# Fifteen more turns by block transposes and DRAM trips in a two-block transformer kernel, and the last down slots by token tile

## What is computed

```python
q, k, v, f_logit = split(h @ w_in)                     # fox_mixer: 16 heads of 128
cum = cumsum(log_sigmoid(f_logit + b_f))
s = (rms_norm(q) @ rms_norm(k).T) * scale + (cum_q - cum_k)
h = h + causal_softmax(s) @ v @ w_out
up = conv3(rms_norm(h) @ w_up); gate, val = split(up)
h = h + (silu(gate) * val) @ w_down                    # width 5632

z = rms_norm(h) @ w_in_2                               # second block
o = hgrn2_scan(silu(hq) * dk**-0.5, 1 - g, hi, log(g)) # 8 heads of 128, g = lb + (1 - lb) * sigmoid(hf)
y_a = rms_norm(o) * silu(hg)
y_b = chunk_band_attention(aq, ak, av, rel_bias)       # 16 heads of 64
merged = gate_a * (y_a @ w_branch_a) + gate_b * (y_b @ w_branch_b)
h = h + merged @ w_out_2
h = h + square(relu(rms_norm(h) @ w_up_2)) @ w_down_2
return rms_norm(h)
```

## Time and profile before

| | us |
|---|---|
| median of 3 runs (lowest, highest) | 2573.26 (2572.63, 2573.35) |
| profiled execution | 2572.82 |
| its span, first to last instruction | 2570.6 |
| PE busy | 2545.2 (99%) |
| DVE busy | 1628.3 (63%) |
| ACT busy | 1274.0 (50%) |
| mean granted TensorE clock | 0.998 of full speed |
| DMA | 530.04 MB, 206 GB/s |

### The profile page before, as it was taken

The page is one execution under the profiler, slowest core; times in us unless marked ns, Lnnn a source line. Parts: engine busy times, 40 slices in busy tenths (PEclk is TensorE's granted clock), DMA queues, the critical chain, the costliest instruction groups (busy, mean ns, idle before and its releaser), DMA issues.

```text
span 2570.6 us, 32628 instructions
## 1 busy us (share of the span) xinstructions
PE 2545.2 (99%) x11604; PEld 2114.7 (82%) x11604; DVE 1628.3 (63%) x1812; ACT 1274.0 (50%) x1609; POOL 173.9 (7%) x289
## 2 busy tenths in 40 slices
PE   8999999999999999999999999999999999999998
PEld 7888888888888888878888888888888888888886
DVE  5666655766666666666677555455565666666665
ACT  5555554655555555554343645454444444444444
POOL 0111100100000000000001000000010000000000
PEclk9999999999999999999999999999999999999999
DMA  7877756877777777755556666665677777777775
GB/s 227 257 204 220 204 170 203 241 225 225 226 223 227 223 223 228 207 170 174 157 151 188 209 194 184 181 191 185 187 238 212 222 211 221 213 219 217 215 219 156
DMA packets 264773, 530.04 MB, mean 206 GB/s; under 512 B 20747, under 2 KB 22131, under 8 KB 264563
## 3 DMA queue, kind: packets, MB, share of 16 engines
q1 hardware_dynamic: 243488, 469.82, 60.7%
q0 software_dynamic: 17152, 54.54, 7.7%
q10 hardware_dynamic: 4051, 4.59, 0.5%
HBM read 501.07 MB, written 27.81 MB: 206 GB/s over the span
## 4 chain that ended last, share of the span: by engine, by line
PE 97%; DVE 1%; DMA 1%; ACT 1%; issue 0%; POOL 0%; ACTq 0%; POOLq 0%; SPq 0%
PE acc L449 31%; PE acc L451 31%; PE acc L450 31%; PE acc L704 1%; PE acc L462 1%; PE acc L557 1%; PE acc L564 0%; DMA scratch<-qk_rows 0%; DVE w_lo L1323 0%; PE acc L579 0%; DVE scratch L1533 0%; DMA raw<-in_w 0%; ACT w_hi L855 0%; PE acc L580 0%; PE acc L741 0%
## 5 line engine op out<-in xcount | busy, mean ns | idle before, releaser
L1323 DVE TENSOR_TENSOR w_lo<-raw,w_hi 128x1024 fp32r<-128x1024 f32 x887 | 1080.4, 1222 | 813.8 <-ACT w_hi L855 811.1
L855 ACT ACTIVATE w_hi<-raw 128x1024 fp32r<-128x1024 f32 x887 | 938.6, 1060 | 1060.3 <-PE acc L451 1001.0
L449 PE MATMUL acc<-w_hi,A_hi 128*128 128x512 f32 x1948 | 769.1, 395 | 0.8 <-issue 0.8
L451 PE MATMUL acc<-w_hi,A_lo 128*128 128x512 f32 x1948 | 758.7, 389 | 0.0
L450 PE MATMUL acc<-w_lo,A_hi 128*128 128x512 f32 x1948 | 758.7, 389 | 0.0
L451 PEld LDWEIGHTS acc<-w_hi,A_lo 128*128 128x128 f32 x1948 | 365.7, 188 | 76.9
L449 PEld LDWEIGHTS acc<-w_hi,A_hi 128*128 128x128 f32 x1948 | 365.9, 188 | 75.8 <-issue 1.4
L450 PEld LDWEIGHTS acc<-w_lo,A_hi 128*128 128x128 f32 x1948 | 365.9, 188 | 73.8
L449 PE MATMUL acc<-w_hi,B_hi 128*128 128x512 f32 x800 | 313.9, 392 | 3.1 <-issue 3.1
L451 PE MATMUL acc<-w_hi,B_lo 128*128 128x512 f32 x800 | 312.1, 390 | 0.0
L450 PE MATMUL acc<-w_lo,B_hi 128*128 128x512 f32 x800 | 311.8, 390 | 0.0
(11 more groups left out here) (184 smaller groups left out, 1240.2 us busy)
## 6 DMA issues: line engine op xcount, KB each, us to landing
raw<-in_up SPq DMA_DIRECT2D x304, 512.0 KB, 4.2
raw<-in_w SPq DMA_DIRECT2D x271, 512.0 KB, 4.1
raw<-in_down SPq DMA_DIRECT2D x216, 512.0 KB, 4.6
raw<-in_wo SPq DMA_DIRECT2D x64, 512.0 KB, 3.9
up_rows<-scratch POOLq DMA_DIRECT2D x21, 512.0 KB, 5.1
scratch<-up_rows POOLq DMA_DIRECT2D x84, 128.0 KB, 5.1
raw<-in_wa SPq DMA_DIRECT2D x16, 512.0 KB, 4.9
raw<-in_wb SPq DMA_DIRECT2D x16, 512.0 KB, 4.7
```

The costliest lines, as they stand in the source:

```text
L449: pe.matmul(o, hi[:, kt, ts], wh, start=first and kk == 0, stop=False)
L451: m = pe.matmul(o, lo[:, kt, ts], wh, start=False, stop=last and kk == SLOT_K - 1)
L855: act.activation(w_hi[:, q % RING, :], raw[:, q % RING, :], ACT.Copy).then_inc(w_hi_ready, 1)
L1323: dve.tensor_tensor(w_lo[:, q % RING, :], raw[:, q % RING, :], f32(w_hi[:, q % RING, :]), ALU.subtract).then_inc(w_lo_ready, 1)
```

## The change

1. Fifteen turns leave PE and go by trips through `turn_rows`: three of the new residual in wo1, the six of the decayed attention, three merged chunks and three of the second residual (`BY_BLOCK`). The sources are ordinary tiles, so DVE cuts the blocks itself, in two transposes of 512 columns (`half_blocks`); POOL sends and reads (`half_send`, `half_bring`, together `half_trip`); `operand_back` on ACT and DVE makes the operand.
2. The steps of the decayed attention are laid out anew (`HG_AT`, `HG_Q`), its y is turned at slots b + 33 (blocks) and b + 43 (operand) instead of b + 34, and the banded attention starts two slots later (`AT_AT`).
3. The score steps of the last four fox heads start at wo1 slots 2, 4, 5 and 7 instead of 1, 3, 5 and 7, with their keys one slot ahead of each.
4. The forget-gate product has hi and lo weights side by side, 32 columns: two matmuls for each k tile instead of three.
5. In the last pass of the first FFN gate steps move forward two slots and value steps one; the last down product takes its banks in another order, and w2's first slots wait for one turned chunk each.
6. The last four slots of the kernel run by token tile: all of tile 0, then all of tile 1, each with its own squares, root, scaling and eight stores of 256 KB instead of four of 512 KB.

The diff, cut to its core (ACT's and DVE's `operand_back` are used at the same slots; the deleted waits on `turned` are left out):

```diff
-        D1_BANKS, D1_TURN, D1_LAST = [BK[2], BK[3], BK[2], BK[3]], [BK[0], BK[3], BK[0], BK[3]], [BK[0], BK[1], BK[0], BK[3]]
+        D1_BANKS, D1_TURN, D1_LAST = [BK[2], BK[3], BK[2], BK[3]], [BK[0], BK[3], BK[0], BK[3]], [BK[1], BK[0], BK[1], BK[3]]
...
+        BY_BLOCK = [TN_RES1 + m for m in range(3)] + [TN_HG + n for n in range(6)] + [TN_MERGE + n for n in range(3)] + [TN_RES2 + n for n in range(3)]
...
+        RES1_AT = [20, 23, 30]
...
-        HG_AT = [18, 54]
-        AT_AT = [93, 137]
+        HG_AT, HG_Q = [21, 56], [15, 54]
+        AT_AT = [95, 139]
...
-            at = {"mix": 5, "turn_p": 3, "score": 1, "turn_qk": 0} if last else \
-                 {"mix": 8, "turn_p": 5, "score": 3, "turn_qk": 1}
+            begun = (2, 4, 5, 7) if last else (3, 5, 7, 9)
+            after = {"mix": 4, "turn_p": 2, "score": 0, "turn_qk": -1} if last else \
+                    {"mix": 5, "turn_p": 2, "score": 0, "turn_qk": -2}
             return [(kind, j) for kind in ("mix", "turn_p", "score", "turn_qk") for j in range(JT)
-                    if p == 2 * j + at[kind]]
+                    if p == begun[j] + after[kind]]
...
-                        pe.matmul(o, fw_hi[:, kt, :], A_hi[:, kt, :], start=kt == 0, stop=False)
-                        pe.matmul(o, fw_lo[:, kt, :], A_hi[:, kt, :], start=False, stop=False)
-                        m = pe.matmul(o, fw_hi[:, kt, :], A_lo[:, kt, :], start=False, stop=kt == KT - 1)
+                        pe.matmul(o, fw[:, kt, :], A_hi[:, kt, :], start=kt == 0, stop=False)
+                        m = pe.matmul(o, fw[:, kt, :], A_lo[:, kt, :], start=False, stop=kt == KT - 1)
...
-                for m in range(NCH - 1):
-                    if p == OUT1_END[m] + 2:
-                        pe.wait_ge(res1_out, m + 1)
-                        pe.wait_ge(mixed_lo, FOX_H)
-                        turn(chunk_of_resid(m), TN_RES1 + m)
...
-            downs(R4 - 2, 0, D1_LAST, [(down1_out, 4 * (FFN1 - 1) - 1), None, (down1_out, 4 * (FFN1 - 1) + 1), (down1_out, 4 * (FFN1 - 1))], (gated, FFN1),
+            downs(R4 - 2, 0, D1_LAST, [None, (down1_out, 4 * (FFN1 - 1) - 1), (down1_out, 4 * (FFN1 - 1) + 1), (down1_out, 4 * (FFN1 - 1))], (gated, FFN1),
...
-                    if kind in ("turn_q", "turn_f"):
-                        f = kind == "turn_f"
-                        pe.wait_ge(z2_out, 4 * g + 1 + f)
-                        turn(halves(stage_k if f else stage_q), TN_HG + 3 * g + f)
...
-                    pe.wait_ge(down1_out, 4 * FFN1 - 1)
-                    pe.wait_ge(turn_dve, TN_DOWN1 + 3)
-                if p == 6:
-                    pe.wait_ge(turn_dve, TN_DOWN1 + 4)
+                    pe.wait_ge(down1_out, 4 * FFN1 - 2)
+                if p in (0, 2, 4, 6):
+                    pe.wait_ge(turn_dve, TN_DOWN1 + p // 2 + 1)
...
+            def last_downs():
+                H = NCH
+                pe.wait_ge(up2_lo, FFN2)
+                for q in range(H):
+                    gemm(R_END - 2, q, A_hi, A_lo, q % 2, D2_LAST[q // 2], q % 2 == 0, q % 2 == 1)
+                pe.wait_ge(down2_out, 4 * FFN2 - 3)
+                for t in range(TT):
+                    for q in range(H, 2 * NCH):
+                        if t == 0:
+                            pe.wait_ge(w_lo_ready, RING * (R_END - 2) + q + 1)
+                        o, ts = acc[:, D2_LAST[q // 2][t], :], slice(t * P, (t + 1) * P)
+                        for kk in range(SLOT_K):
+                            wh, wl = (w[:, q % RING, kk * CW:(kk + 1) * CW] for w in (w_hi, w_lo))
+                            kt, last = q % 2 * SLOT_K + kk, q % 2 == 1 and kk == SLOT_K - 1
+                            pe.matmul(o, A_hi[:, kt, ts], wh, start=q % 2 == 0 and kk == 0, stop=False)
+                            pe.matmul(o, A_hi[:, kt, ts], wl, start=False, stop=False)
+                            m = pe.matmul(o, A_lo[:, kt, ts], wh, start=False, stop=last)
+                        if q % 2 == 1:
+                            m.then_inc(tile_done, 1)
...
+            def operand_back(n, src, hi, kt, g=None):
+                nth = BY_BLOCK.index(n)
+                act.wait_ge(half_back, 64 * (nth + 1))
+                if g is not None:
+                    for j in range(JT):
+                        v = src.rearrange("p (a j e) -> p j a e", a=4, j=JT)[:, j]
+                        m = act.activation(v, v, ACT.Copy, scale=gain[:, g + kt + j:g + kt + j + 1])
+                    chain.link(m)
+                act.activation(in_tokens(hi[:, kt:kt + JT, :]), from_quads(src), ACT.Copy).then_inc(turn_act, 1)
...
-                    if last and p == 2 * SPC - 1:
-                        gate_step(0, i)
+                    if last and p >= 2 * SPC - 2:
+                        gate_step(p - 2 * SPC + 2, i)
...
-                gate_step(q + 1, FFN1 - 1)
+                gate_step(q + 3, FFN1 - 1)
...
+            def operand_back(n, src, hi, lo, kt):
+                dve.wait_ge(turn_act, n + 1)
+                dve.tensor_tensor(in_tokens(lo[:, kt:kt + JT, :]), from_quads(src), f32(in_tokens(hi[:, kt:kt + JT, :])),
+                                  ALU.subtract).then_inc(turn_dve, 1)
+            def half_blocks(n, x, src, ready):
+                nth = BY_BLOCK.index(n)
+                dve.wait_ge(*ready)
+                if nth:
+                    dve.wait_ge(half_sent, 16 * nth)
+                for t in range(TT):
+                    m = dve.transpose(block_columns(x, t), src(t).rearrange("p (j b q) -> p b j q", j=JT, b=4))
+                m.then_inc(half_block, 1)
...
-                    if p == OUT1_END[m] + 2:
-                        operand(TN_RES1 + m, A_hi, A_lo, m * JT, G_FFN)
+                    if p == OUT1_END[m]:
+                        half_blocks(TN_RES1 + m, res1_x, chunk_of_resid(m), (res1_out, m + 1))
+                    if p == RES1_AT[m]:
+                        operand_back(TN_RES1 + m, res1_t[m], A_hi, A_lo, m * JT)
...
-                    if p == b + 34:
-                        operand(TN_HG + 3 * g + 2, B_hi, B_lo, g * JT)
+                    if p == b + 33:
+                        half_blocks(tn_hg(g, 2), y_x[g], lambda t: Z[0][:, t * CW:(t + 1) * CW], (hg_normed, g + 1))
+                    if p == b + 43:
+                        operand_back(tn_hg(g, 2), y_t[g], B_hi, B_lo, g * JT)
+                    for k in range(2):
+                        if p == SPC * (4 * g + k + 1) + 1:
+                            u = (stage_q, stage_k)[k]
+                            half_blocks(tn_hg(g, k), hg_x, lambda t: u[:, t * CW:(t + 1) * CW], (z2_out, 4 * g + k + 1))
...
+                if n and s == 0:
+                    half_blocks(TN_MERGE + n - 1, block_x, lambda t: stage_q[:, t * CW:(t + 1) * CW], (merged_out, n))
+                if n and s == 6:
+                    operand_back(TN_MERGE + n - 1, block_t, A_hi, A_lo, (n - 1) * JT)
...
+            def add_tile(t, c):
+                dve.wait_ge(tile_done, 2 * t + c - 1)
+                v = resid[:, t, c * CW:(c + 1) * CW]
+                dve.tensor_tensor(v, v, acc[:, D2_LAST[c][t], :], ALU.add).then_inc(last_added, 1)
...
+            def finish_tile(t):
+                dve.wait_ge(last_squared, 2 * t + 2)
+                dve.tensor_reduce(ssum[:, t:t + 1], final_ssq[:, t, :], AX_X, ALU.add).then_inc(sums, 1)
+                dve.wait_ge(last_rstd, t + 1)
+                dve.wait_ge(gained, 3 + t)
+                v = resid[:, t, 2 * CW:3 * CW]
+                dve.tensor_scalar(v, v, rstd[:, t:t + 1], None, ALU.mult).then_inc(scaled_dve, 1)
+                v = resid[:, t, 3 * CW:4 * CW]
+                dve.scalar_tensor_tensor(out=v, in0=v, scalar=rstd[:, t:t + 1], in1=gain_out[:, 3 * CW:4 * CW],
+                                         op0=ALU.mult, op1=ALU.mult).then_inc(scaled_dve, 1)
             dve.wait_ge(gain_in, 16)
-            downs(R_END - 2, 0, D2_LAST, down2_out, ahead=False,
-                  steps=lambda q: q in (3, 5) and gain_chunk(q // 2 - 1))
-            gain_chunk(NCH - 2)
-            sum_squares(4)
-            gain_chunk(NCH - 1)
-            dve.wait_ge(rstd_ready, 5)
-            dve.wait_ge(gained, NCH)
...
+            for q in range(NCH):
+                split(R_END - 2, q)
+                if q % 2 == 1:
+                    add_chunk(q // 2, D2_LAST[q // 2], RING * (R_END - 2) + q + 1, down2_out)
+            split(R_END - 2, NCH)
+            gain_chunk(0)
+            gain_chunk(1)
+            add_tile(0, 2)
+            add_tile(0, 3)
+            gain_tile(0)
+            finish_tile(0)
+            add_tile(1, 2)
+            gain_tile(1)
+            add_tile(1, 3)
+            finish_tile(1)
...
+            def half_send(n, x):
+                nth = BY_BLOCK.index(n)
+                pool.wait_ge(half_block, nth + 1)
+                if nth:
+                    pool.wait_ge(half_back, 64 * nth)
+                pool.dma_start(turn_rows, x).then_inc(half_sent, 16)
```

(26 more changed lines are left out.)

230 lines of the change are left out of this document (134 added, 96 removed).

## The result

The changed kernel takes 2588.2 us (median of 10 runs, 2582.5 to 2595.0) against 2573.3 (2571.8 to 2577.4): a ratio of 1.0061, 95% interval 1.0052 to 1.0071. It is slower by 14.9 us, where 2570.0 was forecast. Its runs also lie 12.6 us apart, those of before 5.7. The profiled execution took 2587.03, its span is 2585.2.

What follows compares the result with a forecast made beforehand. PE, busy 2545.2 of 2570.6 us, was taken as the bound. Gains of 21.5 us less 18.2 of added waits gave net -3.3, so 2570.0 us against the median; own range 2564 to 2576, 8 in 10 range 2557 to 2579.

Steps and rivals of the forecast that it cites:

- the reductions: wa/wb and wo2: only each stage's third chunk is tight, with blocks 4 us from slot start; +0.3 us.
- wo1: Residual stage: three trips one behind another make PE idle at the first up-projection slot; +4.5 us, plus +1.5 of clock.
- the tail: Kernel end: storing tile 0 during tile 1's matmuls leaves 9.2 to 10.6 us after the last matmul; gain 2.8 us.
- the bias table: Second attention: `in_rel` lands late behind y's reads, so PE waits for turned probabilities; +8.8 us, plus +1.5 of clock.
- The forecast's own sign of being wrong: Wrong if DVE doesn't wait for `in_rel`, or trip waits appear elsewhere, above all in the two reduction stages.
- Removed from PE: Fifteen turns at 0.79 us, 11.9, and sixteen forget-gate matmuls, 1.9, leave PE: gain 13.8 us, none hidden.
- Seam: First FFN to w2: less PE idle and no clock loss, gain 4.1 us, plus 0.8 in w2's first slot.
- t: Time of one trip of a turned chunk through DRAM: 11 to 15.6 us, taken as 12.6.
- 3t - 33.2: Idle of PE at wo1's slot 32 from three successive trips: 4.6 us at t = 12.6, nothing at 11.
- Score steps and level 0: Last heads' score steps moved: +0.5 us; decayed attention, level 0 work later than PE wants it: +1.1 us.
- Slower than before: Rival 2: DMA queues fill as trips run beside weights, t = 14, table at M + 34.7: 2580 us; chance 0.17.
- rival 3: Everything is covered: no new wait counts, needing table before M + 23 and t under 11; 2552 us; chance 0.06.

Runs made afterwards that it cites:

- 9: Kernel before with only the gate in two matmuls, the seam order, the last down slots by tile and last roots on ACT and DVE: 2561.1 us against 2572.9.
- 12: All-mended kernel with score steps as before the change, two wo1 chunks by trips, operands at slots 20 and 27, third turned by PE: 2550.5 us against 2572.6 before.
- 7: Changed kernel with the last two roots made by ACT and DVE instead of a power on POOL: 2586.6 us against 2573.1 for the kernel before.
- Experiment 4: Changed kernel with operands of the first two chunks of wa/wb and wo2 made three slots later: 2580.2 us against 2573.1 for the kernel before.
- Experiment 2: Changed kernel with the operand of wo1's second residual chunk made four slots later, step 27 instead of 23: 2580.2 us against 2572.9 for the kernel before.
- 5: Changed kernel with POOL issuing `in_rel` ahead of the four reads of y, behind y's send: 2584.7 us against 2573.1 for the kernel before.
- 6: Changed kernel with y's blocks in another buffer, so POOL issues q and k reads, then `in_rel`, then y's trip: 2573.4 us against 2572.9 before.
- 11: All-mended kernel with the last fox heads' score steps where the kernel before has them: 2555.3 us against 2572.6 for the kernel before.
- 1: Changed kernel with wo1's three residual chunks turned by PE again: 2581.7 us against 2573.1 for the kernel before.
- 3: Changed kernel with the third chunks of wa/wb and wo2 turned by PE, the first two still by trips: 2581.4 us against 2573.1 before.
- 10: Changed kernel, all mended: wo1's chunks and third chunks turned by PE, y's trip behind `in_rel`, last roots on ACT and DVE: 2555.1 us against 2572.9 before.

## Why the prediction was wrong, step by step

The forecast was a gain of 3.3, and the traces show a loss of 14.5. Of the 17.8 between them the reductions make 10.1, wo1 4.6, the tail 2.4 and the bias table 2.3; the rest goes the other way, 1.6. The forecast's own sign of being wrong came true: waits for trips in the two reduction stages, "where I gave them almost nothing".

**Removed from PE: right.** 13.8 forecast, 13.9 in the trace. With the stops mended the turns' part reaches the time: from 9 to 12 there are 10.6 us, for twelve turns that are worth 9.5.

**Seam: right, a little low.** -4.9 forecast, -5.9 in the trace. The 0.5 of idle that I left was not there, and the slow slot was 1.7 and not 1.5.

**Tail: the mechanism was right, its end was missing.** I followed the stores and found them at "9.2 to 10.6"; SP was through at 8.5. I had not looked at what follows the stores. The rows of before held it: POOL's DRAIN is a row of the closing line, 8.4 us, and ended 0.2 behind the stores' landing. The step that failed is "what is late next", for the one engine with a long closing instruction. It cost 3.9 (7), and -2.8 became -0.4.

**Reductions (+0.3 forecast, +10.4): the largest error.** Two terms of the same sum were too small. "Blocks need 4 us from the slot's start" was 7.9, because the second chunk's `operand_back` stands on ACT and DVE ahead of the product that is to be cut, and that trip was late itself. And t was 15.3, where I took 12.6. With t = 15.3 and a send at 4 the sum gives -0.2 at wo2; with t = 12.6 and a send at 7.9, 1.0; with both, 3.7, which is what PE stood. Experiment 4 shows the first term nearly alone at wo2: the send is 2.5 earlier, the trip 0.5 shorter, and the stop falls by 3.0. I had allowed the trips to meet nothing but the deadline, and not each other's steps.

**wo1 (+6.0 forecast, +10.6): the chain was right, what it holds up was not.** 3t - 33.2 with the trips of this trace (13.0, 15.1, 13.4) is 8.3. PE's first up slot began 9.2 late by the same count, 6.3 of it idle and 2.8 the slow slot at 27; t was low again. But I put all of it at the first up slot. More than half came at slot 27, where PE needed a split that stood behind ACT's wait. Two stops then cost two slow slots, 4.3 instead of 1.5. The forecast said itself that each engine's steps stand behind the split of their slot, and didn't draw the consequence for a step of ACT that takes, with its wait, longer than the three slots of the split's lead. Nor was the chain a given: the forecast's 7.6 from the second landing to the third send were there only because the second operand's step stood ahead of the third chunk's blocks. Experiment 2 moves that step, and the stops go with trips that are hardly shorter.

**Bias table (+10.3 forecast, +12.6): right, the place and the order of events too.** The wait in front of the first turned probabilities was 9.2 (8.8 forecast). That this single number came so near is luck: the table landed 3.3 later than I took it (M + 35.3, not 32), and the first score's keys, which I had taken as "inside", cost 2.4 of their own and made PE itself later. Experiments 5 and 6 show the causes. With `in_rel` ahead of y's reads the table is there 4.2 earlier. With y's trip behind it as well, the reads begin 7.9 earlier (M + 5.0) and `in_rel` takes 9.3 instead of 13.9, another 12.4. So the larger part is POOL's stand for y's blocks ahead of the reads; how much of the shorter landing belongs to y's bytes, which then come later, was not varied alone.

**Score steps and level 0.** 0.5 and 1.1 forecast, 1.1 and 0.0 in the trace; 11 shows that the first is within noise, and no run varied the second.

**The rivals.** "Slower than before" had the right mechanism, a queue too full beside the weights, with t = 14 and third chunks at 1.5. Its 2580 falls short by what is named above, third chunks (8.9 more) and the tail (2.4), less 1.9 that its bias term was too high and 1.3 in small terms. Its chance of 0.17 was too low. The only two whole trips that I had read took 13.0 and 15.6, and I chose 12.6, below both, from medians of single DMAs. The 3.2 for a send is the median of transfers of the second FFN; in the third chunk's trip the reads begin 5.6 behind the send (1763.22 and 1768.85), and the last landed 8 us behind its issue, not 6.8. In the changed kernel and its variants the residual and reduction trips took 11.7 to 16.2 us.

The estimate from the Trainium skill, page "DMA: Bandwidth & Descriptors", anatomy of a DMA, put a trip under 8 us; no trip here came near that (the shortest in the changed kernel took 9.9), and rival 3 falls with it. By the Trainium skill's page "VectorE: DVE Perf Modes", rules for kernel authors, a 128x128 transpose belongs on TensorE if it may land in PSUM. As the change places the steps, the runs agree for the late chunks (1, 3); with the steps moved, the same chunks by trips cost no more than on PE (2, 4), and for twelve chunks the trips are faster (12 against 9, by 10.6).

## What to carry to other kernels

An engine that waits for a DMA holds back everything behind that step. Before a step with a wait is placed, compare the wait's worst length with the lead of what stands behind it, on every in-order queue (ACT's splits here, POOL's reads), and not only with the deadline of its own result. Move the waiting step late, or give its data another buffer so that the queue can issue the urgent transfer first: three such edits, of a few lines each, took 8.0, 8.0 and 14.8 us off this kernel (2, 4, 6), each by itself and without a single instruction less. And when the end is pulled in, list the closing instructions of all engines: the next one may be right behind.

## What the runs showed of the hardware

- **POOL's closing DRAIN.** It took 9.744 to 9.747 us in the seven kernels whose last POOL operation is the power for one tile's root, 8.4 in the kernel before, and 11.8 to 14.1 in the six whose last POOL instruction is a DMA issue. In the profile it starts 0.03 to 0.3 ahead of the start of that last operation. The other engines' are 0.9 to 2.2 (ACT and DVE) and 4.1 to 4.3 (PE's weight loads).
- **A late DMA issue without a semaphore.** In the changed kernel POOL stood 6.7 us ahead of `in_rel`'s issue, behind thirteen issues that it had made in 8.6 us; in four others with the same order it stood 6.3 to 6.5 (2, 3, 4 and 7). With `in_rel` ahead of the last four (5) it did not stand, and neither did it in 1, behind the same thirteen issues in 8.5 us but with three trips fewer earlier in the kernel. So the number of issues just before is not the cause by itself. What is stays open.
- **The clock behind a stop.** Stops of 2.7 to 6.4 us were followed by a slot that took 1.5 to 2.6 more, at a granted clock of 0.50 to 0.65 in the changed kernel, thus mostly at 1.2 instead of 2.4 GHz; one of 3.2 (in 4, at slot 27 of wo1) cost only 0.15. Stops of 0.9 to 2.2 cost 0.1 to 0.2 there. The stop before the first turned probabilities of the second attention, 4.8 to 9.9 us in seven kernels, cost 0.7 to 2.0; in the changed kernel 1.0 at a granted clock of 0.74.
- **Trips scatter.** The runs of the eight kernels in which PE waits for trips spread over 3 to 15 us (median 10), those of the four without such stops (9 to 12) over 2.5 to 6.3, and before's over 5.7. Four of the eight have 10 or 11 runs and the four have 5 each, which makes some of the difference; with 5 or 6 runs the eight's spreads are 3.4, 6.3, 6.7 and 14.0.
